# Recurrent scan of a bidirectional HGRN2 layer: both differences of a level made by VectorE, GpSimd keeps the query products

## The reference

```python
def step(S, inp):
    qc, kc, vc, gc = inp
    bcs = jnp.cumsum(gc, axis=1)
    o_inter = jnp.einsum('bthk,bhkv->bthv', qc * jnp.exp(bcs), S)
    diff = bcs[:, :, None] - bcs[:, None]
    dec = jnp.exp(jnp.where(mask[None, :, :, None, None], diff, -jnp.inf))
    att = jnp.einsum('bthk,btshk,bshk->bhts', qc, dec, kc)
    o_intra = jnp.einsum('bhts,bshv->bthv', att, vc)
    last = bcs[:, -1]
    S_new = S * jnp.exp(last)[..., None] + jnp.einsum(
        'bshk,bshv->bhkv', kc * jnp.exp(last[:, None] - bcs), vc)
    return S_new, o_inter + o_intra
```

## Time and profile before

| | us |
|---|---|
| median of 3 runs | 2918.61 |
| lowest, highest | 2917.32, 2927.15 |
| profiled execution, its own time | 2921.69 |
| profiled execution, span | 2919.9 |
| stretch of the recurrent scan in it | 1714 to 1891 |

### The profile page before, as it was taken

How to read it: one execution, slowest core, us unless ns; L and a number is a source line. 1 busy time by engine, 2 the same in 40 slices (tenths; PEclk the granted TensorE clock), 3 DMA queues, 4 the chain that set the end, 5 groups by cost and what they waited for, 6 DMA issues and landing times.

```text
span 2919.9 us, 30428 instructions
## 1 busy us (share of the span) xinstructions
PE 2607.6 (89%) x11978; PEld 1912.3 (65%) x11978; DVE 1463.5 (50%) x2105; ACT 747.2 (26%) x1260; POOL 806.6 (28%) x445
## 2 busy tenths in 40 slices
PE   5789899998897889999998877889999899989997
PEld 3678864446896678744458866776444699874444
DVE  6446553335648766633336389974333415650013
ACT  1132230002453442300014344432001334230111
POOL 3355400002443354000014469830000247500000
PEclk7889989998799999899998888898999899979999
DMA  7533649892330215398943411054989143529881
GB/s 267 169 124 101 212 157 347 322 347 71 103 117 30 73 58 174 134 334 316 362 163 136 138 55 36 23 185 148 333 322 348 46 142 101 146 101 302 301 297 41
DMA packets 291853, 524.42 MB, mean 180 GB/s; under 512 B 9472, under 2 KB 141056, under 8 KB 291328
## 3 DMA queue, kind: packets, MB, share of 16 engines
q1 hardware_dynamic: 288256, 519.33, 51.4%
q10 hardware_dynamic: 3456, 3.15, 0.3%
HBM read 517.73 MB, written 4.72 MB: 179 GB/s over the span
## 4 chain that ended last, share of the span: by engine, by line
PE 75%; DVE 12%; ACT 4%; issue 3%; DMA 3%; POOL 2%; SPq 0%; ACTq 0%; DVEq 0%
PE ps L1865 23%; PE ps L1880 11%; PE ps L1615 6%; PE ps L1616 6%; PE ps L1617 6%; PE ps L1680 3%; DVE macc L1952 2%; POOL wlo L1547 2%; DVE uw L1308 1%; PE ps L1638 1%; PE ps L1804 1%; PE ps L1639 1%; PE ps L1640 1%; PE ps L1828 1%; PE ps L1829 1%
## 5 line engine op out<-in xcount | busy, mean ns | idle before, releaser
L1547 POOL TENSOR_TENSOR wlo<-ring,whi 128x1024 fp32r<-128x1024 f32 x202 | 528.6, 2633 | 1488.1 <-ACT whi L1414 1487.9
L1865 PE MATMUL ps<-ring,xg 128*128 128x512 f32 x1536 | 706.4, 604 | 0.0
L1865 PEld LDWEIGHTS ps<-ring,xg 128*128 128x128 f32 x1536 | 289.7, 194 | 328.7 <-issue 328.3
L1952 DVE SCALAR_TENSOR_TENSOR macc<-ring,cond_s,macc 128x1024 f32<-128x1024 f32 x322 | 435.6, 1413 | 10.4 <-DMA ring<-w_mod 10.4
L2170 DVE SCALAR_TENSOR_TENSOR hid<-ps,cws,sg 128x256 f32<-128x256 f32 x96 | 46.4, 484 | 671.4 <-ACT sg L1508 671.4
L1880 PE MATMUL ps<-ring,hidt 128*128 128x512 f32 x768 | 350.0, 599 | 2.3 <-ACT hidt L1483 2.3
L1615 PE MATMUL ps<-hh,whi 128*128 128x384 f32 x832 | 304.0, 365 | 27.0 <-POOL wlo L1547 20.6
L1616 PE MATMUL ps<-hl,whi 128*128 128x384 f32 x832 | 291.4, 350 | 0.0
L1617 PE MATMUL ps<-hh,wlo 128*128 128x384 f32 x832 | 291.4, 350 | 0.0
L1414 ACT ACTIVATE whi<-ring 128x1024 fp32r<-128x1024 f32 x202 | 207.1, 1054 | 298.9 <-DMA ring<-gmlp_w_out 110.8
L1880 PEld LDWEIGHTS ps<-ring,hidt 128*128 128x128 f32 x768 | 147.5, 193 | 187.4 <-issue 187.4
(11 more groups left out here) (352 smaller groups left out, 4159.8 us busy)
## 6 DMA issues: line engine op xcount, KB each, us to landing
ring<-moe_w_gu SPq DMA_DIRECT2D x192, 1024.0 KB, 7.5
ring<-w_mod SPq DMA_DIRECT2D x96, 1024.0 KB, 8.2
ring<-moe_w_down SPq DMA_DIRECT2D x96, 1024.0 KB, 5.1
ring<-gmlp_w_in SPq DMA_DIRECT2D x32, 1024.0 KB, 5.9
ring<-ssd_w_in SPq DMA_DIRECT2D x21, 1024.0 KB, 5.3
ring<-hgrn_w_in SPq DMA_DIRECT2D x20, 1024.0 KB, 5.4
ring<-gmlp_w_out SPq DMA_DIRECT2D x16, 1024.0 KB, 5.7
ring<-ssd_w_out SPq DMA_DIRECT2D x8, 1024.0 KB, 5.8
```

The costliest lines, as they stand in the source:

```text
L1547: pool.tensor_tensor(split_sub(wlo, s0), raw_sub(s0), split_sub(whi, s0).bitcast(F32), ALU.subtract).then_inc(S["lo_ready"], 1)
L1865: ins = pe.matmul(ps[:, s % 2, :], xg[:, w, k, :], whole(what, s, 4)[:, k % 4, :], start=(k == 0), stop=(k == KD - 1))
L1952: ins = dve.scalar_tensor_tensor(out=macc[:, v, :], in0=w[:, k, :], scalar=by, in1=macc[:, v, :], op0=ALU.mult, op1=ALU.add)
```

## The change

VectorE makes both differences of a level, one behind the other, and signals `u_sub` once, behind the second. GpSimd's `decay` and the semaphore `w_sub` go; ScalarE waits for `u_sub` alone. GpSimd's query products, `hqe` and `wlo` stay in their order. The operands of the moved difference are the same.

```diff
                 for j in range(LEVELS):
                     n = LEVELS * h + j
                     act.wait_ge(S["u_sub"], n + 1)
-                    act.wait_ge(S["w_sub"], n + 1)
                     uw = uw_slot(n)
                     act.activation(uw[:, :, :], uw[:, :, :], ACT.Exp).then_inc(S["u_exp"], 1)
...
             pool.wait_ge(S["scan_ready"], 16)
             pool.wait_ge(S["q_evac"], 8)
-            def decay(n):
-
-                h, j = n // LEVELS, LEVELS - 1 - n % LEVELS
-                if n >= 3:
-                    pool.wait_ge(S["lv_done"], step_of(n - 3) + 1)
-                out = uw_slot(n)[:, 1, :].rearrange("p (b two x) -> p b two x", two=2, x=1 << j)
-                pool.tensor_tensor(out, crossed(h, j), border(h, j, True), ALU.subtract).then_inc(S["w_sub"], 1)
-
-            decay(0)
             for n in range(LEVELS * HH):
                 h, j = divmod(n, LEVELS)
-                if n + 1 < LEVELS * HH:
-                    decay(n + 1)
                 pool.wait_ge(S["u_exp"], n + 1)
                 W = uw_slot(n)[:, 1, :]
                 pool.tensor_tensor(W, W, hq[:, h, :], ALU.mult).then_inc(S["wq_ready"], 1)
...
                 if g >= 3:
                     dve.wait_ge(S["lv_done"], step_of(g - 3) + 1)
                 out = uw_slot(g)[:, 0, :].rearrange("p (b two x) -> p b two x", two=2, x=1 << j)
-                dve.tensor_tensor(out, border(h, j), paired(hf_flat, h, j), ALU.subtract).then_inc(S["u_sub"], 1)
+                dve.tensor_tensor(out, border(h, j), paired(hf_flat, h, j), ALU.subtract)
+                out = uw_slot(g)[:, 1, :].rearrange("p (b two x) -> p b two x", two=2, x=1 << j)
+                dve.tensor_tensor(out, crossed(h, j), border(h, j, True), ALU.subtract).then_inc(S["u_sub"], 1)
```

More of the change, by code:

```diff
@@ L349, in trunk @@
         hst_out = [sem(f"hst_out{d}") for d in range(2)]
-        names = """cols_in x_in consts_set hi_ready lo_ready sub_done w_sub wq_ready mac_step pe_mod_used mod_row mod_summed mod_read cond_ready
+        names = """cols_in x_in consts_set hi_ready lo_ready sub_done wq_ready mac_step pe_mod_used mod_row mod_summed mod_read cond_ready
             h32_ready hh_ready hl_ready y_ready mean_done diff_ready sq_ready sq_added var_done std_ready norm_ready x_ready
```

## The result

The changed kernel takes 2936.32 us in the median (2934.83 to 2937.16, 5 runs), the kernel before 2918.61 (2914.70 to 2927.15, 5 runs beside them). The ratio is 1.0046, with a 95% interval of 1.0025 to 1.0067. I had forecast 2917, no change; the range ended at 2930. A second set of runs gave 1.0049 (1.0026 to 1.0072). So the change costs close to half a per cent: by the ratio some 14 us, while the two medians lie 17.7 us apart.

The account below looks back on a forecast made before the run. The exclusive SBUF port was taken to pace each scan head. Seven heads from 22.2 to 22.0 us (-1.4) and +0.5 at the start gave about -1 us, 2917 on the median's scale; range 2904 to 2930.

Parts of the forecast that it names:

- The exclusive port: Recurrent scan: VectorE and GpSimd instructions with two SBUF operands exclude each other; this paces a head, 21.9 of 22.23 us.
- the bound without overlap: Changed head if none of GpSimd's port time lies beside VectorE's picks, copies and carries: 24.0 us, plus waits.
- The sum of 21.9: Port time per head before the change: VectorE 6.6 plus GpSimd 15.3 us, against 22.23 in the trace.
- The price of the moved difference: Each difference moved to VectorE was to cost 0.43 us at the port and 0.47 in its queue.
- 14.9 us of own work: VectorE's own queue per head after the change: differences, products, keys, copies, carries and picks; 11.6 us before.
- the 90% that was to be kept: Sign in the changed kernel: VectorE should stay above 90% busy.
- The overlap of 2.4: Per changed head, 2.4 us of GpSimd's port time lies beside VectorE's picks, copies and carries, of 4.2 at most.
- The wait: VectorE stands 0.4 us a head for ScalarE's late exponential, which blocking covered before the change.
- The walk: VectorE's order followed through one changed head to count overlap: sum 2.2, taken as 2.4 us.
- wlo feeds gate products that TensorE takes a head later, so it gains nothing: GpSimd's queue in the scan: the seven low halves stand earlier and meet a freer engine, with no gain.
- The slower rival: VectorE's queue becomes the bound, GpSimd's product blocking each second difference: 23.9 us a head, 2932 us; chance 0.15.
- The faster rival: The port goes on pacing the scan, overlap 4.2: heads of 19.8 to 20.5 us, typically 2905 us; chance 0.22.

Follow-up runs that it names:

- e13: Changed kernel with VectorE's product of the level before made between the two differences, not behind them; 2945.46 us, ratio 1.0050 to the kernel before.
- e6: Kernel before with the scan's seven low halves (`wlo`) cut to 16 of 1024 columns; 2911.34 us, one run.
- e12: e8 with GpSimd's query product also cut to 16 of 384 columns; 2910.22 us, one run.
- e2: Kernel before with the low half issued one level earlier on GpSimd; 2941.76 us, ratio 1.0067 to the kernel before.
- e8: Changed kernel with VectorE's product of level 6 made ahead of the two differences; 2933.41 us, ratio 1.0029 to the kernel before.
- e1: Changed kernel with GpSimd's low half moved behind both products of the next head's level 0; 2926.00 us, ratio 1.0001 to the kernel before.
- e5: Changed kernel with the scan's seven low halves cut to 16 of 1024 columns; 2919.63 us, one run.
- after: The changed kernel, both differences on VectorE, first set of runs; 2936.32 us, ratio 1.0046 to the kernel before.
- r1: The changed kernel run a second time, nothing altered; 2938.81 us, ratio 1.0049 to the kernel before.

## Why the prediction was wrong, by its own steps

**The exclusive port** is right as a mechanism: VectorE's and GpSimd's instructions with two operands in SBUF alternate in every run here, and e13 meets the bound without overlap to 0.1 us. Wrong was that it alone paces a head of the kernel before. The sum of 21.9 fitted 22.23, in part by luck: the five heads hold 1.6 us of waiting at diagonal picks, for which the sum has no place, VectorE was idle 0.56 a head over the six, and taking 2.25 us off that sum (e6) shortened the head by 1.5 only.

**The price of the moved difference** (0.43 at the port, 0.47 in the queue) fit: L1291 is recorded like L1289, and 14.9 us of own work agrees with both e12 and e13, though neither measures it by itself. GpSimd's idle time went to ScalarE, as foretold, and its busy time fell to 92.27 in the scan, where 95 was said. VectorE was busy 169.93 of 189.42 us there, 89.7%, just under the 90% that was to be kept.

**The overlap of 2.4** was about right for the changed kernel: 24.0 less 2.4 is 21.6 of busy time, and 21.83 was measured.

**The wait** is the step that failed: "VectorE also stands 0.4 for the late exponential" is the only waiting in the sum. VectorE stood 2.45, of which about 0.5 for the exponential, as said, and 1.8 before the diagonal pick, for which the sum has no term. The walk had the low half in its true place, blocking the second of a pair for its whole 2.25, and charged it with that; it did not ask what is queued behind the blocked difference. That is the product of level 6, and TensorE's chain from there to the diagonal result took 4.87 at a granted clock of 0.61 (4.7 to 5.7 over the six heads), where in the kernel before it took 3.1 at 1.00 in the head shown. Over the six heads of the kernel before it took 3.1 to 5.7, but only one chain was as long as 5.7. What was waited beyond the 0.4 is 1.9 to 2.1 us a head (2.27 and 2.45 less 0.4), over six heads 11 to 12, against a loss of 12.8 in the scan (13.8 in the six heads, the first and the last together 0.9 the other way). Two runs show the wait to hang on the start of the chain: it comes with the low half's place in the other kernel (e2) and goes when the product is made first (e8). e1 shows that the low half's place is what the loss in time hangs on, but takes away mostly blocking (1.0 of 1.76 a head) and only 0.3 of the 1.8 before the pick.

**"wlo feeds gate products that TensorE takes a head later, so it gains nothing"** asked only who needs the result. Nobody needed it earlier; but a step that comes earlier also blocks earlier.

**The slower rival** had nearly the right time (2932, 4 us more with no overlap) by another mechanism. The product that falls between the two differences is real (e8, e13), but in the changed kernel most of the loss was the wait. The two are not independent: take the wait away and blocking takes up part of it, so that e8 gave back 1.1 of 2.3 and e1, which lessened both, 1.8. Their shares in the 2.3 us can be given by difference of runs only (1.3 with the low half, 1.0 without it), not as a sum of causes.

**The faster rival** priced its gain at "1.1 to 2.4 a head"; from its own heads of 19.8 to 20.5 against 22.2 it would be 1.7 to 2.4. Heads of that length appeared in e5, with the low half cut short, where the chain ran at 1.00.

What stays open: why the clock fell before some chains and not before others with the same idle time in front, and what the changed kernel would take with the clock held. The length of the chain and the wait go with the clock in every head of after, r1 and e1, but no run held the clock fixed.

## What to carry to other kernels

When work is taken off an engine, write down what it now does earlier, not only what it no longer does: its remaining long instructions move, and on a port used by one engine at a time they may move in front of the one instruction that a third engine waits for. In such a sum, count for each blocked instruction who is queued behind it and how long the chain behind that is, at both levels of TensorE's clock that the trace shows for it (3.1 and 5.7 us here). And two orders with the same sum are not the same kernel: one digit in the place of an instruction of 2.25 us cost 1.8 us a head (1.35 against the second execution of the kernel before).

## What the runs showed of the hardware that I had not expected

The exclusion of VectorE and GpSimd can become a fixed rhythm: in e13 every head from the second to the seventh took 24.68 to 24.70 us, with GpSimd's products in the same places, to 0.04 us, each time.

TensorE's chain of 25 instructions took 3.10 us at a granted clock of 1.00, after 1.06 us of idle time, and 4.87 at 0.61, after 3.63. The first three microseconds and more of it ran at 0.50, the lower level, 1.2 GHz, as the table of stretches has it:

```profile
1843.13:1846.50 3.37, 3.32 (x14) 3.32 (x15) 3.24 (x6) 1.64 (x5) 1.14 (x2) 0.50 0.00 0
1846.50:1848.00 1.50, 1.50 (x13) 1.50 (x13) 0.00 (x0) 0.00 (x0) 0.85 (x1) 0.85 0.00 0
```

All eighteen chains behind 3.16 to 3.64 us of idle time began below the upper level; behind 1.05 to 1.49 us there were chains at 1.00 and at 0.50, of the same kernel. A delay in front of TensorE can thus cost more than itself: the lower level made a chain of 3.1 us one of up to 5.7.
